# Reading the moving weights of the expert gate and up matmuls in another column order

## What is computed

```python
def swiglu(h, w_gate, w_up, w_down):
    return (jax.nn.silu(h @ w_gate) * (h @ w_up)) @ w_down

top_logit, top_idx = lax.top_k(logits, TOP_K)        # 2 of 8 experts for each token
gates = jax.nn.softmax(top_logit, axis=-1)
# tokens sorted by expert into padded blocks of 128 rows, one expert for a block:
yb = lax.map(expert_block, (buf.reshape(n_blocks, MOE_BLOCK, D), block_exp))
y = yb.reshape(cap, D)[dest] * sorted_gate[:, None]
out = jax.ops.segment_sum(y, sorted_tok, num_segments=n)
```

## Time and profile before

| | |
|---|---|
| median of 3 runs | 1404.3 us |
| the profiled execution, its time | 1404.85 us |
| the profiled execution, its span | 1402.6 us |
| mean granted TensorE clock | 0.996 |
| TensorE busy with matmuls | 1386.5 us, 99% |
| VectorE busy | 1138.9 us, 81% |
| ScalarE busy | 935.4 us, 67% |
| read from and written to HBM | 429.74 MB and 18.36 MB |

### The profile page before, as it was taken

One profiled execution on the slowest core, in us unless ns is written; L12 is line 12 of the kernel. 1 busy time (PEld: TensorE's weight loads), 2 busy tenths in 40 slices (PEclk: granted clock), 3 DMA queues, 4 the chain that ended last, 5 costly groups with the idle time before them and its releaser, 6 DMA issues.

```text
span 1402.6 us, 19224 instructions
## 1 busy us (share of the span) xinstructions
PE 1386.5 (99%) x7367; PEld 1181.9 (84%) x7367; DVE 1138.9 (81%) x861; ACT 935.4 (67%) x752; POOL 36.5 (3%) x52
## 2 busy tenths in 40 slices
PE   8999999999999999999999999999999999999997
PEld 7888999889888888888888888888888888888885
DVE  5866665546857999988888888898888889889897
ACT  5565444345555777777877777777777777777775
POOL 0010000000010020000000000000000000001200
PEclk9999999999999999999999999999999999999998
DMA  9734985555434999999999999999999999999993
GB/s 335 261 120 131 394 326 201 182 178 187 156 99 158 346 399 393 396 394 397 373 395 385 365 386 391 379 367 390 393 350 396 382 370 387 393 375 362 395 395 120
DMA packets 190910, 448.85 MB, mean 320 GB/s; under 512 B 8515, under 2 KB 11402, under 8 KB 190858
## 3 DMA queue, kind: packets, MB, share of 16 engines
q1 hardware_dynamic: 188890, 441.74, 85.8%
q0 software_dynamic: 1648, 5.78, 1.1%
q10 hardware_dynamic: 320, 0.60, 0.1%
HBM read 429.74 MB, written 18.36 MB: 319 GB/s over the span
## 4 chain that ended last, share of the span: by engine, by line
PE 98%; DVE 1%; ACT 0%; DMA 0%; issue 0%; DVEq 0%; ACTq 0%
PE ps L535 91%; PE ps L992 2%; PE ps L664 1%; PE ps L622 1%; PE ps L695 0%; PE ps L951 0%; PE ps L718 0%; PE ps L653 0%; DMA cst<-in_consts 0%; PE ps L540 0%; PE ps L683 0%; PE ps L962 0%; PE ps L678 0%; PE ps L684 0%; PE ps L665 0%; PE ps L606 0%
## 5 line engine op out<-in xcount | busy, mean ns | idle before, releaser
L385 DVE TENSOR_TENSOR w_lo<-raw,w_hi 128x2048 fp32r<-128x2048 f32 x401 | 915.0, 2291 | 184.6 <-ACT w_hi L380 183.6
L380 ACT ACTIVATE w_hi<-raw 128x2048 fp32r<-128x2048 f32 (+1 forms) x401 | 767.5, 1916 | 295.2 <-PE ps L535 292.5
L535 PE MATMUL ps<-w_hi,xe_hi 128*128 128x512 f32 x896 | 244.7, 395 | 0.0
L535 PE MATMUL ps<-w_hi,xe_lo 128*128 128x512 f32 x896 | 240.0, 390 | 0.0
L535 PE MATMUL ps<-w_lo,xe_hi 128*128 128x512 f32 x896 | 239.9, 389 | 0.0
L535 PEld LDWEIGHTS ps<-w_hi,xe_lo 128*128 128x128 f32 x896 | 168.2, 188 | 35.9
L535 PEld LDWEIGHTS ps<-w_lo,xe_hi 128*128 128x128 f32 x896 | 168.2, 188 | 35.5
L535 PEld LDWEIGHTS ps<-w_hi,xe_hi 128*128 128x128 f32 x896 | 164.6, 188 | 31.6
L535 PE MATMUL ps<-w_hi,he_hi 128*128 128x512 f32 x448 | 120.9, 391 | 0.0
L535 PE MATMUL ps<-w_lo,he_hi 128*128 128x512 f32 x448 | 120.3, 390 | 0.0
L535 PE MATMUL ps<-w_hi,he_lo 128*128 128x512 f32 x448 | 120.1, 389 | 0.0
(11 more groups left out here) (248 smaller groups left out, 961.5 us busy)
## 6 DMA issues: line engine op xcount, KB each, us to landing
raw<-in_expert_w_gate SPq DMA_DIRECT2D x112, 1024.0 KB, 7.6
raw<-in_expert_w_up SPq DMA_DIRECT2D x112, 1024.0 KB, 7.9
raw<-in_expert_w_down SPq DMA_DIRECT2D x112, 1024.0 KB, 7.7
raw<-in_w_in SPq DMA_DIRECT2D x24, 1024.0 KB, 6.5
raw<-in_dense_w_gate SPq DMA_DIRECT2D x11, 1024.0 KB, 6.9
raw<-in_dense_w_up SPq DMA_DIRECT2D x11, 1024.0 KB, 7.9
raw<-in_dense_w_down SPq DMA_DIRECT2D x11, 1024.0 KB, 5.0
raw<-in_w_out SPq DMA_DIRECT2D x8, 1024.0 KB, 5.3
```

Of the source, the lines that this page charges most:

```text
L380: nc.scalar.activation(half_of(w_hi, n, first), raw[:, n % RAW, first:PIECE], ACT.Copy).then_inc(hi_ready, 1)
L385: nc.vector.tensor_tensor(half_of(w_lo, n), raw[:, n % RAW, :], half_of(w_hi, n).bitcast(F32), ALU.subtract).then_inc(lo_ready, 1)
L535: return pe.matmul(o, stationary, moving, start=start, stop=stop, skip_group_check=True)
```

## The change

The moving operand of the gate and up matmuls is read in another order: columns 0 to 15, 256 to 271, 16 to 31, 272 to 287 and so on, in place of 0 to 511 in turn. A run of 16 columns is 64 bytes in a partition, and the two halves are 1024 bytes apart. The output bank is written from its first to its last column as before (its view has the same four dimensions and is contiguous), so the gate and up results lie in PSUM in the new order. Silu is applied in that order. VectorE's multiplication puts the columns back into their places when it writes `hid`, in runs of 16. The down matmuls, the dense layer, both projections, all loads, all waits and all instruction counts are as before.

```diff
+LINE = 16
@@ TensorE, expert_in @@
-                    o = ps[:, (0 if kind == "gate" else 2) + c % 2, :]
+                    o = ps[:, (0 if kind == "gate" else 2) + c % 2, :].rearrange("p (a h c) -> p a h c", h=2, c=LINE)
+
+                    def halves_in_turn(w, k):
+                        return w[:, k * CH:k * CH + CH].rearrange("p (h a c) -> p a h c", h=2, c=LINE)
+
                     for k in range(4):
-                        add(o, xe_hi[:, 4 * half + k, :], hi[:, k * CH:k * CH + CH], start=(half == 0 and k == 0))
+                        add(o, xe_hi[:, 4 * half + k, :], halves_in_turn(hi, k), start=(half == 0 and k == 0))
                     for k in range(4):
-                        add(o, xe_lo[:, 4 * half + k, :], hi[:, k * CH:k * CH + CH])
+                        add(o, xe_lo[:, 4 * half + k, :], halves_in_turn(hi, k))
                     lo = low(n, b)
                     for k in range(4):
-                        last = add(o, xe_hi[:, 4 * half + k, :], lo[:, k * CH:k * CH + CH], stop=(half == 1 and k == 3))
+                        last = add(o, xe_hi[:, 4 * half + k, :], halves_in_turn(lo, k), stop=(half == 1 and k == 3))
@@ VectorE, expert_block @@
-                        V.tensor_tensor(hid[:, (c - 1) % 2, :], sil[:, (c - 1) % 2, :], ps[:, 2 + (c - 1) % 2, :],
+                        V.tensor_tensor(hid[:, (c - 1) % 2, :].rearrange("p (h a c) -> p a h c", h=2, c=LINE),
+                                        sil[:, (c - 1) % 2, :].rearrange("p (a h c) -> p a h c", h=2, c=LINE),
+                                        ps[:, 2 + (c - 1) % 2, :].rearrange("p (a h c) -> p a h c", h=2, c=LINE),
                                         ALU.mult).then_inc(ehid_done, 1)
```

## The result

The changed kernel takes 1440.1 us (median of 4 runs, 1439.01 to 1440.89) against 1404.17 us for the kernel before on the same chip (4 runs, 1403.84 to 1405.83). The ratio is 1.0254, 95% interval 1.0242 to 1.0265: slower by 36 us. The forecast was no change; the time lies at the price of the third rival, 1440.1 us, which had a chance of 0.12 and was left out of the range.

What follows compares the result with a forecast made beforehand. TensorE was taken as the bound, through the number of matmuls by the distance between starts. Three terms of 0 left 1404.85 us, less 0.55 for the median: 1404.3 us, range 1367 to 1418 us.

Steps and rivals of the forecast that it cites:

- third rival: Gate and up matmuls: each of 32 breaks in the moving read adds a cycle; +35.8 us, 1440.1 us; chance 0.12.
- Term 1: Distance between starts of the 2688 gate and up matmuls: no change, 0.0 us, with ends -35.8 and +35.8 kept.
- Term 2: VectorE's multiplication into `hid`, written in 64-byte runs: any extra pass hidden, 0.0 us; at most 30 us without cover.
- Term 3: PSUM reads by Silu and the multiplication, and TensorE's writing: contiguous as before, 0.0 us, no other end.
- First rival: Gate and up moving reads: alternating places hides the surplus cycle between neighbouring 64-byte runs; -35.8 us, half -17.9; chance 0.28.
- Second rival: Gate and up matmuls: moving read meets the next weight load; 8.9 us more, or 23.8 in its dear form; chance 0.15.

Runs made afterwards that it cites:

- one_col: Kernel before, but gate matmuls read one column 512 times and up matmuls read columns 256 to 511 before 0 to 255; 1389.5 us, ratio 0.9896.
- run64: Changed kernel with runs of 64 columns in turn from the two halves in place of 16; 1404.2 us, ratio 1.0000 to the kernel before.
- run32: Changed kernel with runs of 32 columns in turn from the two halves in place of 16; 1429.6 us, ratio 1.0181 to the kernel before.
- out_turns: Kernel before, weights read contiguously, but the output bank written in turn in its two halves, 16 columns each; 1404.18 us, ratio 0.9995.
- rows_on16: Kernel before with 64 bytes of empty space in front of the experts' stationary tiles, weights where they were; 1428.38 us, ratio 1.0164.
- both_back: Kernel before with expert weights begun 64 bytes earlier and stationary tiles moved by 448 bytes; 1403.77 us, ratio 0.9997.
- narrow_plain: Kernel before with only 64 of the 128 stationary columns used in gate and up, contiguous order; 1412.62 us, ratio 1.0053.
- same16: Kernel before, but each gate and up matmul reads the first 16 columns of its tile 32 times; 1443.66 us, ratio 1.0275.

## Why the prediction was wrong

**What bounds the kernel: right.** TensorE without gaps, everything else waiting for it, cost carried by the distance alone. Rows after confirm each item, and the price of a changed distance (13.3 ns x 2688 = 35.8 us) is what was paid: 36 us in the medians.

**Term 1, the distance: this is the step that failed.** I took "no change" because the surplus of one cycle in 16 was the same for weights and `aT`, at 256 and 512 columns, "which is how a limit on the rate of columns behaves, and less how a clash of particular addresses behaves". one_col refutes the premise: on the same stationary tiles, at the same clock, 512 columns take 518 cycles when the address stands still. And what the step put at nothing was 32 cycles or 13.3 ns a matmul, from reading the moving operand in short runs (run64 544, run32 568, the changed kernel 576). The steadiness in my rows came with what those operands shared: all were contiguous, and the expert pieces lay at the start that costs least of the four tried (the starts of the `aT` tiles were not varied). A regularity over tiles that share the order and the placement tells nothing about an order they do not have. I had written that no row shows a broken run; that should have moved chance away from "no change" to both sides, and the range should not have left out an end that I had kept in the working.

**Term 2, `hid`: right.** 681 ns against 680, and no new idle time before the transposes.

**Term 3, PSUM: right.** The output was contiguous as before, and out_turns shows that even an output in turns costs nothing.

**First rival, faster: wrong in sign, half right in substance.** The surplus goes when the address stands still (one_col), so it is tied to addresses, as this rival supposed, but alternating between two places adds to it, at 1024 bytes and at 128.

**Second rival, two reads meet: the mechanism exists, but not as the cause.** rows_on16 and both_back show it in the contiguous order, at 16 cycles. In the new order 576 cycles stand with either start and with half the load, so I found no share of the 32 that depends on it; other starts were not tried. What I had held against this rival, that the distance is exact in spite of ever-changing slots, was no argument: a slot is 2176 elements or 8704 bytes, 17 x 512, the tiles inside a piece are 2048 bytes apart and the stationary tiles 512, so every matmul has the same relative start modulo 512 bytes, and both_back shows that a shift of 512 bytes changes nothing. The pace that I gave the weight load fits narrow_plain: 64 columns fewer shorten it by 54 ns, 0.84 ns a column, where the moving read takes 0.44.

**Third rival, each jump costs a cycle: the right time by a law that is wrong.** That it hit 1440.1 us is luck: at 32 jumps, and at no other number tried, its law and the measured cost meet. The reader does pay for short contiguous runs, but not once for each jump.

**What stays open.** The runs fix that the cost depends on run length (free at 256 bytes, 24, 32, 40 and 56 cycles at 128, 64, 32 and 16), and that it lies in reading and not in writing. In each of them a weight load runs beside every matmul, so none shows the moving read by itself. They do not show what in the reader makes it so, why it grows by 8 cycles from 128 to 64 and from 64 to 32 bytes but by 16 to the next, why exchanging neighbours costs 16 to 24, or why half a weight load makes the contiguous order slower by 9. Nor did any run look into the slower stretch of 256 columns (117.8 ns) from which the prediction took a bound. No version beat the kernel before: both_back equals it (0.9997), and one_col, the only faster one, leaves the work out.

## What to carry to other kernels

When TensorE is the bound, look at the distance between starts against columns over clock, and compare it with a matmul that reads a single column: what goes then belongs to the moving operand and not to the number of columns. As far as these runs reach, keep the moving operand of fp32r matmuls in contiguous runs of 256 bytes or more, and put a reordering that is needed on the output in PSUM instead, where runs of 64 bytes cost nothing. When a tile is moved, even by padding in front of it, compare the distance before and after: 64 bytes cost 16 of 544 cycles here, 24 us in all.

## What the runs showed of the hardware that I had not expected

A matmul of 512 fp32r columns has a distance of 215.8 ns if it reads one column over and over, 226.7 ns contiguously at best, 233.3 ns contiguously at a bad start against the stationary tiles, and 240.0 ns in runs of 64 bytes. The Trainium skill ("TensorE: Matmul & The Clock Gate", section "Wait — 56ns, not 53.3ns?") has 215.7 ns for 512 columns, in a passage whose example is bf16; the prediction weighed it as a possible gain of 29.5 us, and one_col, on fp32r, agrees with it. The costs of placement and of short runs do not add up: together they give the larger one. Going back to a 64-byte piece that was just read costs about as much as going on to a new one (same16, about 580 cycles against 576).
